# A two-block network on one core: the residual and its norms with features on partitions

## The reference, cut to what matters

```python
def rmsnorm(x, g):
    x32 = x.astype(jnp.float32)
    y = x32 * lax.rsqrt(jnp.mean(x32 * x32, axis=-1, keepdims=True) + EPS)
    return (y * g.astype(jnp.float32)).astype(x.dtype)

def modulate(h, shift, scale):
    return h * (1 + scale) + shift

def swiglu(h, w1, w3, w2):
    return (jax.nn.silu(h @ w1) * (h @ w3)) @ w2
...
        # first block, layer i (0: attention and Fourier mixer, 1: convolution mixer)
        mod_l = jnp.split((silu_c @ ada_w[i] + ada_b[i])[:, None, :], 6, axis=-1)
        h_l = modulate(rmsnorm(x, mix_norm_g[i]), mod_l[0], mod_l[1])
        ...
        x = x + mod_l[2] * y_l
        x = x + mod_l[5] * swiglu(modulate(rmsnorm(x, ffn_norm_g[i]), mod_l[3], mod_l[4]),
                                  ffn_w1[i], ffn_w3[i], ffn_w2[i])
    return rmsnorm(x, final_g)
...
    # second block: a gated linear recurrence, then attention with shared keys and values
    for layer in range(DEPTH):
        shift, scale, gate = jnp.split(cs @ mod_w[layer] + mod_b[layer], 3, axis=-1)
        h = _modulate(_rmsnorm(x, norm_g[layer]), shift, scale)
        if layer < N_A_LAYERS:
            y = _rglru_mixer(h, ...)      # u, g = split(h @ w_in); conv; gates; scan; (hs * silu(g)) @ w_out
        else:
            k_sh, v_sh, km_sh = _shared_kv(x, cs, kv_norm_g, kv_mod_w, kv_mod_b, w_kv)
            y = _moba_mixer(h, k_sh, v_sh, km_sh, ...)   # (softmax(q k) v * silu(g)) @ w_out
        x = x + gate[:, None, :] * y
    return _rmsnorm(x, final_norm_g)
```

## Time and profile before

| | us |
|---|---|
| median of 3 runs | 1105.89 |
| lowest, highest | 1105.78, 1108.47 |
| profiled execution | 1112.0 |
| its span | 1110.3 |
| PE busy (matmuls) | 980.9 (88%) |
| DVE busy | 804.5 (72%) |
| ACT busy | 483.3 (44%) |
| POOL busy | 89.3 (8%) |

### The profile page before, as it was taken

The page is one execution under the profiler, slowest core; times in us unless marked ns, Lnnn a source line. Parts: engine busy times, 40 slices in busy tenths (PEclk is TensorE's granted clock), DMA queues, the critical chain, the costliest instruction groups (busy, mean ns, idle before and its releaser), DMA issues.

```text
span 1110.3 us, 12913 instructions
## 1 busy us (share of the span) xinstructions
PE 980.9 (88%) x4541; PEld 785.2 (71%) x4541; DVE 804.5 (72%) x1221; ACT 483.3 (44%) x772; POOL 89.3 (8%) x123
## 2 busy tenths in 40 slices
PE   4699988688999999799878999999958968899986
PEld 0588854566888888678756788888847856777765
DVE  0596757688777777899978777777778397875554
ACT  1442236434344333466463344333344684535452
POOL 0000100010001000000004000100010210100000
PEclk8799989998999999899988899999979989999988
DMA  8797750067988889423205498888835335684000
GB/s 329 263 347 263 246 192 1 14 227 246 308 302 282 288 297 309 149 81 109 76 14 214 131 351 306 278 295 290 302 127 174 130 126 177 227 304 152 1 1 38
DMA packets 115438, 221.11 MB, mean 199 GB/s; under 512 B 6984, under 2 KB 63281, under 8 KB 115393
## 3 DMA queue, kind: packets, MB, share of 16 engines
q1 hardware_dynamic: 95089, 142.35, 37.1%
q0 software_dynamic: 20304, 78.19, 20.7%
HBM read 219.47 MB, written 1.05 MB: 199 GB/s over the span
## 4 chain that ended last, share of the span: by engine, by line
PE 69%; DVE 15%; ACT 7%; issue 3%; DMA 3%; POOL 1%; SPq 1%; POOLq 0%; DVEq 0%; ACTq 0%
PE bank L1615 18%; PE bank L1617 18%; PE bank L1616 18%; DVE w_lo L971 4%; PE bank L1991 3%; PE bank L1691 3%; ACT w_hi L544 2%; DVE job_sum L988 1%; PE bank L2027 1%; DMA w_land<-ev_w_in_dram 1%; PE bank L1672 1%; DVE tmp L1053 1%; DVE x L1054 1%; PE bank L1824 1%; PE bank L1929 1%
## 5 line engine op out<-in xcount | busy, mean ns | idle before, releaser
L1615 PE MATMUL bank<-w_hi,xT_hi 128*128 128x512 f32 x816 | 336.7, 413 | 27.0 <-DVE xT_lo L1076 14.1
L971 DVE TENSOR_TENSOR w_lo<-w_land,w_hi 128x2048 fp32r<-128x2048 f32 x124 | 283.1, 2288 | 95.6 <-ACT w_hi L544 95.4
L1617 PE MATMUL bank<-w_hi,xT_lo 128*128 128x512 f32 x816 | 326.2, 400 | 0.0
L1616 PE MATMUL bank<-w_lo,xT_hi 128*128 128x512 f32 x816 | 325.8, 399 | 0.0
L544 ACT ACTIVATE w_hi<-w_land 128x2048 fp32r<-128x2048 f32 x124 | 236.8, 1913 | 141.5 <-PE bank L1617 128.9
L1615 PEld LDWEIGHTS bank<-w_hi,xT_hi 128*128 128x128 f32 x816 | 158.9, 195 | 67.3 <-issue 22.1
L1617 PEld LDWEIGHTS bank<-w_hi,xT_lo 128*128 128x128 f32 x816 | 157.8, 193 | 34.7
L1616 PEld LDWEIGHTS bank<-w_lo,xT_hi 128*128 128x128 f32 x816 | 159.0, 195 | 32.0 <-issue 1.0
L988 DVE SCALAR_TENSOR_TENSOR job_sum<-a_land,silu_c,job_sum 128x1024 f32<-128x1024 f32 x126 | 164.2, 1303 | 9.5 <-DMA a_land<-ada_w_dram 4.5
L1615 PE MATMUL bank<-w_hi,hT_hi 128*128 128x512 f32 x176 | 69.9, 397 | 0.0
L1617 PE MATMUL bank<-w_hi,hT_lo 128*128 128x512 f32 x176 | 68.8, 391 | 0.0
(11 more groups left out here) (265 smaller groups left out, 1110.6 us busy)
## 6 DMA issues: line engine op xcount, KB each, us to landing
w_land<-ffn_w_dram SPq DMA_DIRECT2D x132, 512.0 KB, 5.7
a_land<-ada_w_dram POOLq DMA_DIRECT2D x40, 1024.0 KB, 5.8
a_land<-mod_w_dram POOLq DMA_DIRECT2D x24, 1024.0 KB, 5.7
w_land<-od_pw_w_dram SPq DMA_DIRECT2D x24, 512.0 KB, 5.5
w_land<-ev_w_in_dram SPq DMA_DIRECT2D x20, 512.0 KB, 13.1
w_land<-ada_w_dram SPq DMA_DIRECT2D x16, 512.0 KB, 10.8
a_land<-kv_mod_w_dram POOLq DMA_DIRECT2D x8, 1024.0 KB, 6.5
w_land<-rg_w_in_dram SPq DMA_DIRECT2D x16, 512.0 KB, 6.2
```

The source lines that it names most:

```text
L971: dve.tensor_tensor(w_lo[u % N_SPLIT][:, :], w_land[n % N_LAND][:, :], w_hi[u % N_SPLIT][:, :].bitcast(F32), ALU.subtract).then_inc(s_lo, 1)
L1615: pe.matmul(dst, hi, whi, start=start, stop=False)
L1616: pe.matmul(dst, hi, wlo, start=False, stop=False)
L1617: return pe.matmul(dst, lo, whi, start=False, stop=stop)
```

## The change

The residual is kept as `xT`, features on partitions (128 x 8 x 256).

- `by_channel`: in 66 of the 124 units (out, the down half of both FFNs, pw1, pw2, rg_in, rg_out, the k half of kv, att_in, att_out) the weights are stationary and the activations move, 256 columns: 48 matmuls of 128x256 per unit in place of 24 of 128x512. The result has features on partitions. The transposes of pw1, rg_in, k and q go, and the copies ahead of them.
- `channel_residual`: one DVE instruction per feature tile (128x256), with the gate as a column. `gate_diag`, `gate_mm`, `gate_copy` go.
- The norm: `squares` on ACT (128x256 each), `token_sums` on PE (squares stationary, a column of ones moving, 16 calls of 128x1), the mean on DVE, one power on POOL, `rstd_diag` on DVE, `rstd_rows` on PE (ones times the diagonal, 128x256), `stream_operand` on DVE and `stream_hi` on ACT, for both token tiles at once. In n_rg the end norm of block one is folded in: squares and sums are made twice (`sq`, `sq_g`); x itself is multiplied later, after rg_in's first chunk. The norm of q reuses the rows of the norm of k and v (`rb_keep`).
- Attention: the probabilities are scaled ahead of their transpose, the product gives features on partitions, and the gate is made with tanh inside the loop, as are `ao_hi` and `ao_lo` of all heads but two.
- The end: PE multiplies `xT` by a diagonal of the last gain (f32), which turns it; ACT and DVE scale halves of the rows into `result`.
- pw2's bias: eight steps on ACT in place of POOL's four.
- Start: all small loads are issued on ACT's queue, 14 of them ahead of silu(c); the copies of `ada_rows` come ahead of the first `split_hi`, and `split_lo(0)` behind the modulation columns; x is transposed before ada unit 4.

```diff
+            def squares(stage, ks, g=None):
+
+                for k in ks:
+                    act.wait_ge(*seen("xres", stage, k + 1))
+                    act.activation(sq[:, k, :], xT[:, k, :], ACT.Square).then_inc(sem("sq"), 1)
+                    if g is not None:
+                        act.activation(sq_g[:, k, :], xT[:, k, :], ACT.Square, scale=g(k)).then_inc(sem("sq"), 1)
...
+            def stream_hi(stage, full, hi, shift):
+
+                for k in range(KT):
+                    act.wait_ge(*seen("full", stage, k + 1))
+                    act.activation(hi[:, k, :], full[:, k, :], ACT.Identity, bias=mc(shift, k, 1)).then_inc(sem("hi"), 1)
...
+            load_rows(0)
+            act.dma_start(ident[:, :], t_in["k_ident"]).then_inc(sem("ident_in"), 16)
+            load_rows(1)
...
-            split_hi(0)
-            split_hi(1)
...
             act.wait_ge(sem("ada0_used"), ADA0 // 2)
             act.activation(ada_rows[:, 0, :], bank[0][:, :], ACT.Copy).then_inc(sem("ada0_rows"), 1)
             act.wait_ge(sem("ada0_used"), ADA0)
             act.activation(ada_rows[:, 1, :], bank[1][:, :], ACT.Copy).then_inc(sem("ada0_rows"), 1)
+            split_hi(0)
+            split_hi(1)
...
-            def gate_diag(stage, col, dst=None):
-
-                g = (gate if dst is None else dst)[:, :].rearrange("p (k f) -> p k f", k=KT)
-                dve.tensor_tensor(g, ident[:, :].unsqueeze(1).broadcast_to([P, KT, P]),
-                                  col.unsqueeze(2).broadcast_to([P, KT, P]), ALU.mult).then_inc(sem("diag"), 1)
...
-            def residual(c, t, b, wait):
...
-                link(dve.tensor_tensor(part, bank[b][:, :], gate[:, cols], ALU.mult))
-                dve.tensor_tensor(x[:, t, cols], x[:, t, cols], part, ALU.add).then_inc(sem("xres"), 1)
+            def channel_residual(after, k, place, gate_col, wait):
+                b, e = place(k)
                 dve.wait_ge(*wait)
+                dve.scalar_tensor_tensor(out=xT[:, k, :], in0=bank[b][:, 256 * e:256 * e + 256], scalar=gate_col[:, k:k + 1],
+                                         in1=xT[:, k, :], op0=ALU.mult, op1=ALU.add).then_inc(sem("xres"), 1)
...
+            def token_means(stage):
+                dve.wait_ge(*seen("ssum", stage, 1))
+                dve.tensor_scalar(ms[:, 0:NT], bank[S_BANK[stage]][:, 0:NT], 1.0 / D, EPS, ALU.mult, ALU.add).then_inc(sem("ms"), 1)
...
+            def rstd_diag(stage, r, n=1):
+                dve.tensor_tensor(rdiag[:, :, :], ident[:, :].unsqueeze(1).broadcast_to([P, NT, P]),
+                                  r.unsqueeze(2).broadcast_to([P, NT, P]), ALU.mult).then_inc(sem("rdiag"), 1)
+                dve.wait_ge(*seen("rbc", stage, n))
...
+            def stream_operand(stage, full, hi, lo, shift, rb):
+                def low(k):
+                    dve.wait_ge(*seen("hi", stage, k + 1))
+                    dve.scalar_tensor_tensor(out=lo[:, k, :], in0=full[:, k, :], scalar=mc(shift, k, 1),
+                                             in1=hi[:, k, :].bitcast(F32), op0=ALU.add, op1=ALU.subtract).then_inc(sem("lo"), 1)
+                for k in range(KT):
+                    dve.scalar_tensor_tensor(out=full[:, k, :], in0=xT[:, k, :], scalar=a_col[:, k:k + 1], in1=rb,
+                                             op0=ALU.mult, op1=ALU.mult).then_inc(sem("full"), 1)
+                    if k >= 1:
+                        low(k - 1)
+                low(KT - 1)
...
+            def by_channel(u, j, dst, start, hi, lo, ready=None, ks=range(4), ms=range(4), blocks=False, marks=()):
+                wh = w_hi[u % N_SPLIT][:, :].rearrange("p (k n) -> p k n", k=4)
+                wl = w_lo[u % N_SPLIT][:, :].rearrange("p (k n) -> p k n", k=4)
+                order = [(k, m) for m in ms for k in ks] if blocks else [(k, m) for k in ks for m in ms]
+                for n, (k, m) in enumerate(order):
+                    kt = 4 * j + k
+                    if ready is not None and m == ms[0]:
+                        pe.wait_ge(*seen("lo", ready, min(kt + 1, ADDS[ready]["lo"])))
+                    ins = three(dst(m), wh[:, k, m * P:m * P + P], wl[:, k, m * P:m * P + P], hi[:, kt, :], lo[:, kt, :],
+                                kt == 0 and start(m), kt == KT - 1 and (m % 2 == 1 or start(m + 1)))
+                    if blocks and k == ks[-1] and m in marks:
+                        ins.then_inc(sem("part"), 1)
+                return ins
...
+            def token_sums(stage, ks, twice=False):
+                b = bank[S_BANK[stage]]
+                tiles = (sq, sq_g) if twice else (sq,)
+                for k in ks:
+                    for n, src in enumerate(tiles):
+                        pe.wait_ge(*seen("sq", stage, len(tiles) * k + n + 1))
+                        for t in range(NT):
+                            ins = pe.matmul(b[:, 2 * n + t:2 * n + t + 1], src[:, k, t * P:t * P + P], ones[:, 0:1],
+                                            start=(k, n, t) == (0, 0, 0), stop=(k, n, t) == (KT - 1, len(tiles) - 1, NT - 1))
+                    if k == KT - 1:
+                        ins.then_inc(sem("ssum"), 1)
...
+            def rstd_rows(stage, n=1, b=6):
+                pe.wait_ge(*seen("rdiag", stage, n))
+                pe.matmul(bank[b][:, 0:S], ones[:, :], rdiag[:, :, :].rearrange("p t s -> p (t s)"), start=True,
+                          stop=True).then_inc(sem("rbc"), 1)
...
+            def dense(stage, ready, after, hi, lo, turn_out=None):
+                u = BASE[stage]
+                def dst(g):
+                    b, e = block_place(g)
+                    return bank[b][:, 256 * e:256 * e + 256]
+                for j in range(2):
+                    unit_wait(u + j)
+                    by_channel(u + j, j, dst, lambda m: m % 2 == 0, hi, lo, ready).then_inc(s_used, 1)
+                late, firsts = (lambda m: dst(m + 4)), (lambda m: m != 1)
+                unit_wait(u + 2)
+                by_channel(u + 2, 0, late, firsts, hi, lo).then_inc(s_used, 1)
+                unit_wait(u + 3)
+                by_channel(u + 3, 1, late, firsts, hi, lo, None, range(4), (0, 1, 2), True, (1, 2))
+                token_sums(after, range(6))
+                if turn_out is not None:
+                    turn_out(range(4))
+                by_channel(u + 3, 1, late, firsts, hi, lo, None, range(4), (3,), True).then_inc(s_used, 1)
+                if turn_out is not None:
+                    turn_out(range(4, 6))
+                token_sums(after, range(6, KT))
+                if turn_out is not None:
+                    turn_out(range(6, KT))
...
+            rstd_diag("n_rg", rstd[:, 0:2], 2)
+            for k in range(KT):
+                dve.scalar_tensor_tensor(out=xT[:, k, :], in0=xT[:, k, :], scalar=pc("final_g", k), in1=bank[5][:, 0:S],
+                                         op0=ALU.mult, op1=ALU.mult).then_inc(sem("x_final"), 1)
```

900 lines of the change are left out of this document (376 added, 524 removed).

## The result

The changed kernel takes **1129.5 us** in the median of four runs (1128.0 to 1132.0), the kernel before 1107.2 beside it (1105.8 to 1109.3): ratio **1.0177, 95% interval 1.0148 to 1.0207**. It is slower by some 20 us, where 29 us less had been forecast, and it lies outside the range. The profiled execution is 1128.0 (span 1126.3) against 1112.0 (1110.3) before, +16.0; the remaining few us are that the profiled run of before was a high one.

The account below looks back on a forecast made before the run. PE was taken to bound the long stages, with serial chains between them. Nine terms summed to -28.9 us, taking the median from 1105.9 to 1077, own range 1066 to 1088 (chance 0.60), with ends at 1063 and 1101.

Parts of the forecast that it names:

- What bounds the kernel: Whole kernel: PE bounds the long stages; between them PE waits for short serial chains on other engines.
- Start: Kernel start: ada copies first and small loads on ACT's queue bring the first main product to about 39.9; -4.0 us.
- Stream: Matmuls of 66 units: 256 columns lie 0.114 us apart, about four fifths where PE is the bound; +1.0 us.
- rival A: Split matmuls: the 14 ns are paid per matmul, 0.121 us each, +18 us, so 1095; chance 0.15.
- Norm boundary at out: Norm after out: shorter chain and no transposes, but PE waits about 2 us for squares; +1.0 us, ends -2 and +4.
- pw1 and layer norm: pw1 boundary, GLU transposes and layer norm's end: few transposes on the path, eight steps get shorter; -2.5 us.
- pw2: pw2: gate and bias gate spreads and POOL's bias steps go; -4.4 us, ends -1 and -7.
- rg: rg stages: folded end norm and fewer transpose waits, against DVE's multiply by the end norm; -3.9 us, rg_out -0.4.
- k, v and q: Chunks of k and q: waits and transposes go, as does q's norm turning, with 2.2 taken back; -7.5 us.
- Attention's end: Attention loop's end to last store: gating, turning of ao and gate spreads go, PE's end work adds 1.5; -8.2 us.
- C: Norm boundaries: chains don't shorten because of queues and the falling clock; 15 us given back, 1092; chance 0.13.
- B: Split matmuls: weight loads become the bound; at 136 ns each +56 us, 1133, deciding from 0.125 apart; chance 0.12.

Follow-up runs that it names:

- the mended kernel: The changed kernel with w_lo quartered in the attention loop, the end norm's multiply later and token sums behind the last block: 1104.1 us, ratio 0.9945.
- the quarters: The changed kernel with the attention loop's three w_lo splits cut into quarters of 512 columns, one after each of twelve rounds: ratio 1.0099.

## Why the prediction was wrong, point by point

- **What bounds the kernel**: right. PE, with serial chains between the stages.
- **Start** (-4.0): right in sum, and partly by luck. The first main product comes at 39.65 against the 39.9 of the text, 4.2 us earlier, and the whole start put into the kernel before gave 4.0. But the two parts of the sum were both wrong and made up for each other. The copies first were counted as 2.8 and cost 3.5 by themselves, since PE reaches the fifth unit before its weights. The queue was counted as 1.2, and is worth 6.5 to 10.5 us in three comparisons (6.5 in the mended kernel, 7.5 in the kernel before with the copies first, 10.5 in the changed kernel). The step that failed looked at SP's first weights (2.3 us) only, and not at the second place that the diff touches, where SP issues small loads for 13.4 us between two groups of weights:

```profile
36.04 2.10 SPq L378 DMA_DIRECT2D rope<-k_rope_dram  x1
...
49.44 10.88 SPq L303 DMA_DIRECT2D w_land<-ev_w_in_dram  x10
```

  The issue time that mattered was this 13.4 us, and what the queue was worth stays below it. The Trainium skill (Trainium Kernel Development and Optimization, Key Constraints) says that issuing from several engines saves only issue time; these runs agree with that.
- **Stream** (+1.0): wrong, and it was a term's size. 0.120 apart instead of 0.114, which is rival A. The argument against A, that f32 matmuls show no 14 ns, was the step that failed: their rows are of another type, and the fp32r row at 512 columns was the nearest. The run with all 66 units cut puts the price at +9, not A's +18; the likely reason is that the 44 units outside the FFNs lie mostly in stages that wait for DVE or ACT. "Four fifths" was too much: 9.4 of at most 1584 x (0.240 - 0.2275) = 19.8 is about half. The Trainium skill (TensorE: Matmul & The Clock Gate, Back-to-back issue gap) gives some 2.5 ns on top of the columns, which would have made +4 by an estimate. The fp32r products here don't agree: they show 13 to 14 ns at the full clock.
- **Norm boundary at out** (+1.0, ends -2 and +4): +4.7, above the upper end. The 2 us of waiting ahead of the last block were named, and came (2.04). What was left out is that PE then goes on at half the clock: the sums in 1.87 instead of 0.92, the block, and the chain's small matmuls. The run with the sums moved gives some 8 us for their place in all boundaries.
- **pw1 and layer norm** (-2.5): +4.2; 1.1 with the mends. In the taps' stage DVE is busy 67.05 of 67.16 us before: it is the bound, so PE's transposes cost nothing there, and what DVE had ahead of it only moved in.
- **pw2** (-4.4): right, -5.0. The gates and POOL's bias steps were on the path and are gone.
- **rg** (-4.3 with rg_out): the second FFN's end and the gates give +9.0. The text had the very row, DVE's multiply by the end norm "ahead of job and w_lo", and it counted 3.9 us of DVE work and 3.6 of waiting on PE for it. The work was 3.23 and the wait for the w_lo 2.30, so neither was too small. The step that failed is a term put at nothing: the multiply itself waits for a PE product behind rg_in's first two units, and DVE stood idle for 6.59 us. From it come the second wait, 3.44 for the job's sums, and the half clock behind both. Putting the multiply some 25 us later brings 12 us.
- **k, v and q** (-7.5): -0.7 for the whole stretch from rg's gates to q. The waits between the chunks are gone, as forecast. In their place stand the price of 256 columns in rg_out and in the k and q units, a new wait of 3.8 us where q's operand is made anew, a wait of 9.56 for 6.80 ahead of rg_out, and a clock of 0.92 for 0.96:

```profile
1000.89 0.55 PE L1562 MATMUL bank<-xT_hi,w_hi 128*128 128x256 f32 x1 [3.80 <-DVE xT_lo L1022]
```

- **Attention's end** (-8.2): +8.4 (13.0 - 0.5 - 4.1). The gain is there: the first product of att_out follows the last head at once, where before 6.3 us (1068.30 to 1074.60) of gating and transposes lay between. The loop gives it back twice. The step of the prediction that failed is "What covers the added steps: ACT and DVE have room in every stage that is counted": the loop's new DVE steps were put at nothing, because DVE was busy only half of it (22.65 of 42.98 us). But a step between ACT's exponential and PE's transpose can be on the path whatever DVE's share, and behind a 2.29 us w_lo it is 3 us late. Of the 13.0 the quarters take back 7.7; 5.3 stay.
- **Rivals**: A's spacing came with half its price; C ("DVE's queue stands ahead of the residual steps, PE stands ahead of its last block, and the clock falls in the wait") named the mechanism, and was taken as 3 us at five boundaries, 15 in all. At the boundaries it was 8; the 12 at the end norm and the 9 in the loop are the same kind of delay at two places that C doesn't name: 26 by the run with all three. B, the load, did not happen: at the full clock the spacing is 0.120, below the 0.125 from which B decides. So the kernel is slower, as B alone had it (0.12), but not by B's way.

The account, in ratios times 1107: the changed kernel +19.6. Less the order on the queues, -25.7, gives -6.1 (the mended kernel). Of that the loads and the start are -4.0 (measured on the kernel before) to -6.5 (the loads alone, on the mended kernel). What is left, 0 to -2, is the smaller products against what the shorter chains bring: if the products cost the +9 that they cost in the kernel before, the chains bring 9 to 11. The forecast had 26 us for these chains. How much of the missing 15 to 17 lies in the half clock and how much in waits that remain (the loop's 5, q's 4) isn't told apart by any run.

## What to carry over

Price an instruction by what stands behind it on its engine and by what it waits for itself, not by its length. Ask of each step that a change puts in a queue whose next work it delays; and if it waits for another engine, ask what stands ahead of its source there (6.59 us here, for a step of 3.23). An engine's busy share doesn't answer either question. Put short steps on PE's path ahead of weight splits, or cut the splits, and never leave PE's finished weights behind a sum that isn't ready. Waits in front of PE can be paid twice, since the work behind them may begin at half the clock, as it did behind waits of 2.04, 2.30 and 3.44 us here. Before counting a gain at the start of a stream, look at which queue issues the next load and what stands ahead of it.
